# Second block's attention: two weight roundings and their rests moved from the differential heads' steps to the 64-wide heads' steps

## The reference, cut to what matters

```
proj = n @ w_in                           # then split into the parts of three kinds of heads
o_a = mla_causal_attention(...)           # 6 heads, 64 + 32 wide
o_b = diff_causal_attention(...)          # 6 heads, each with two softmaxes over 32-wide halves
o_b = rmsnorm(o_b, sub_norm) * (1 - lam)  # needs all six of them
o_c = moba_causal_attention(...)          # 4 heads, 64 wide; 256 tokens are one block
o = concatenate([o_a, o_b, o_c])
h = h + o @ w_out                         # w_out is 1024 x 1024
h = h + memory_cross_attention(...)       # its keys and values come from another input, mem
```

## Time and profile before

| | us |
|---|---|
| median of 3 runs | 2760.85 |
| lowest and highest | 2758.65, 2761.04 |
| span of the profiled execution | 2767.1 |
| PE busy in it | 2704.7 (98%) |
| DVE busy | 1978.5 (72%) |
| ACT busy | 1665.1 (60%) |

### The profile page before, as it was taken

One profiled execution on the slowest core, in us unless ns is written; L12 is line 12 of the kernel. 1 busy time (PEld: TensorE's weight loads), 2 busy tenths in 40 slices (PEclk: granted clock), 3 DMA queues, 4 the chain that ended last, 5 costly groups with the idle time before them and its releaser, 6 DMA issues. The chain is left out here.

```text
span 2767.1 us, 38903 instructions
## 1 busy us (share of the span) xinstructions
PE 2704.7 (98%) x15424; PEld 2291.4 (83%) x15424; DVE 1978.5 (72%) x2069; ACT 1665.1 (60%) x1965; POOL 86.5 (3%) x86
## 2 busy tenths in 40 slices
PE   8999999999999999999999999999999999999998
PEld 5878999788988888888888888889768998867897
DVE  4756655586779998989899898986655555474555
ACT  3575444558467777777777777766445445354544
POOL 1000100110001000000000000011000000000000
PEclk8999999999999999999999999999999999999999
DMA  9847854865579999999999999986424544414452
GB/s 346 299 139 273 321 203 146 278 226 198 172 289 385 393 377 378 377 374 379 380 374 375 381 373 376 378 276 194 142 92 146 189 183 136 170 62 153 183 190 77
DMA packets 317754, 718.08 MB, mean 260 GB/s; under 512 B 7990, under 2 KB 26916, under 8 KB 317620
## 3 DMA queue, kind: packets, MB, share of 16 engines
q1 hardware_dynamic: 311488, 697.99, 69.5%
q0 software_dynamic: 5520, 18.02, 2.0%
q10 hardware_dynamic: 612, 0.18, 0.0%
HBM read 697.28 MB, written 18.87 MB: 259 GB/s over the span
## 5 line engine op out<-in xcount | busy, mean ns | idle before, releaser
L2775 DVE TENSOR_TENSOR ring_rest<-ring,weights_hi 128x2048 fp32r<-128x2048 f32 x270 | 607.5, 2284 | 9.7 <-ACT weights_hi L2100 7.3
L2100 ACT ACTIVATE weights_hi<-ring 128x2048 fp32r<-128x2048 f32 x270 | 516.6, 1916 | 131.9 <-PE ps L1833 75.7
L1831 PE MATMUL ps<-weights_hi,xg_hi 128*128 128x512 f32 x1008 | 400.9, 398 | 0.7 <-DVE xg_lo L2775 0.7
L1833 PE MATMUL ps<-weights_hi,xg_lo 128*128 128x512 f32 x1008 | 395.0, 392 | 0.0
L1832 PE MATMUL ps<-ring_rest,xg_hi 128*128 128x512 f32 x792 | 310.2, 392 | 0.0
L2100 ACT ACTIVATE arena<-ps 128x512 f32<-128x512 f32 (+6 forms) x307 | 157.3, 529 | 220.0 <-PE ps L1833 54.1
L1852 PE MATMUL ps<-weights_hi,hidden_split_moe 128*128 128x512 f32 x1008 | 284.1, 393 | 1.3 <-DVE hidden_split_moe L2775 1.1
L2775 DVE TENSOR_TENSOR w_split<-ring,w_split 128x1024 fp32r<-128x1024 f32 x128 | 150.9, 1221 | 154.5 <-ACT w_split L2100 154.5
L2775 DVE TENSOR_TENSOR ring_rest<-ring,mix_hi 128x2048 fp32r<-128x2048 f32 (+2 forms) x76 | 173.4, 2284 | 117.2 <-ACT mix_hi L2100 116.7
L2775 DVE TENSOR_TENSOR late_rest<-arena,weights_hi 128x2048 fp32r<-128x2048 f32 x108 | 244.5, 2286 | 5.3 <-ACT weights_hi L2100 4.3
L2100 ACT ACTIVATE weights_hi<-arena 128x2048 fp32r<-128x2048 f32 x108 | 207.0, 1917 | 62.3 <-PE ps L1833 32.5
(11 more groups left out here) (310 smaller groups left out, 5289.5 us busy)
## 6 DMA issues: line engine op xcount, KB each, us to landing
ring<-in_moe_w_gate_dram SPq DMA_DIRECT2D x54, 2048.0 KB, 10.1
ring<-in_moe_w_up_dram SPq DMA_DIRECT2D x45, 2048.0 KB, 10.1
ring<-in_moe_w_down_dram SPq DMA_DIRECT2D x36, 2048.0 KB, 9.2
ring<-in_mlp_w_dram SPq DMA_DIRECT2D x32, 2048.0 KB, 8.8
arena<-in_moe_w_down_dram SPq DMA_DIRECT2D x27, 2048.0 KB, 9.9
ring<-in_w_mod_dram SPq DMA_DIRECT2D x48, 1024.0 KB, 8.8
ring<-in_w_in_dram SPq DMA_DIRECT2D x48, 1024.0 KB, 6.2
arena<-in_moe_w_up_dram SPq DMA_DIRECT2D x18, 2048.0 KB, 10.4
```

The costliest lines, as they stand in the source:

```text
L1831: pe.matmul(b, xg_hi[:, k, :], hi[:, i, :], start=(k == 0), stop=False)
L1833: mm = pe.matmul(b, xg_lo[:, k, :], hi[:, i, :], start=False, stop=(k == KD - 1))
L2100: return act.activation(o, i, func, **kw)
L2775: return dve.tensor_tensor(o, a, b, op)
```

## The change

The two first roundings and rests are issued later in the same loops. Nothing is added or taken away.

```
 # ACT, L2199
-                    if b == 2 and s in (4, 6):
-                        round_2(l, O2_0 + s // 6)
+                    if b == 2 and s in (7, 9):
+                        round_2(l, O2_0 + s // 9)
 # DVE, L2911
-                    if b == 2 and s in (5, 7):
-                        rest_2(l, O2_0 + s // 7)
+                    if b == 2 and s in (8, 10):
+                        rest_2(l, O2_0 + s // 10)
```

## The result

The changed kernel takes 2765.32 us (median of 16 runs, 2761.09 to 2771.94), the kernel before 2760.61 us (16 runs, 2757.01 to 2764.89). The ratio is 1.0017, with a 95% interval of 1.0009 to 1.0024: 4.7 us slower, between 2.5 and 6.6. Forecast were +4.4 us and 2765.3 us, within 0.2% of no change.

A forecast was written before the change was run, and what follows sets the result against it. PE, busy 98% of the span, was taken to bound the kernel. Gain 0 from leaving steps 4 to 7 and 2.2 us cost per layer made 2760.85 + 4.4 = 2765.3 us; range 2758 to 2770.5.

The forecast's parts named there:

- Leaving steps 4 to 7: Taking roundings off ACT in steps 4, 6 and rests off DVE in 5, 7: gain 0, O(3) still waits 0.79 us.
- the fall: PE's granted clock drops from 2.4 to 1.2 GHz after the wait in step 6; priced at 3.14 us per layer.
- The 0.4 us kept for the range: Possible gain per layer at O(4) in step 7, from PT(4)'s copy, only where the clock does not fall.
- The wait at O(7): Step 9's second rounding on ACT delays the copy of PT(7), so PE newly waits 0.98 us at O(7).
- PT(10) 1.8 and O(9) 2.18 us late: Steps 11 and 12, after the second rest on DVE: PT(10) waits 0.85 us more, O(9) is 2.18 us late in all.
- Nothing gives it back: From step 13 on nothing absorbs the delay of about 2 us; distances stay as before from scores(13) on.
- The sum: Both layers' attentions: 2.2 us slower per layer, +4.4 us in all, giving 2765.3 us.
- The 6.3 us between span and median: Median of three runs below the profiled span by 6.3 us, put down to profiler overhead and that execution's clock.
- Rival 1: New waits in steps 10 to 12 make PE's clock fall once more per layer: 6.3 us on top, 2771.6; chance 0.12.
- Rival 2: Step 6's wait goes and the clock stays up: 7.9 us faster, 2753.0, or 2757.4 with the new waits; chance 0.10.
- Rival 3: Everything arriving in steps 7 to 10 finds room, as DVE idles 28% of the span: 0, 2760.9 us; chance 0.16.

The follow-up runs named there:

- the filling: Kernel before, with PE's filling in steps 6, 7, 8, 9, 12, 14, 16, 17 instead of 7, 8, 9, 10, 12, 14, 16, 17: 2756.36 us, ratio 0.9982.
- the small matmuls: Kernel before, with seven more 128 x 128 matmuls on PE in step 6, in front of the wait for O(3): 2757.66 us, ratio 0.9989.
- the rests alone: Kernel before, with only the rests moved, to steps 8 and 10, and the roundings kept in steps 4 and 6: 2762.21 us, ratio 1.0007.
- the roundings behind the copy: Changed kernel, with ACT's roundings of steps 7 and 9 behind their step's copy of PT(s-2): 2761.09 us, ratio 1.0006 to the kernel before.

## Why the prediction was right

**Leaving steps 4 to 7: 0.** Right. O(3) waits 0.80 us in the changed kernel against 0.79, released by ACT, and scores(6) to scores(8) are 11.04 us against 11.05. The rounding and the rest that had stood next to the wait had no part in it; the fall went with the edits on PE, the filling and the small matmuls.

The 0.4 us kept for the range rests on more than the rounding that I named. With the rests alone, layer 1 had no fall and the rounding still in step 6, in front of PT(4)'s copy:

```profile
2438.96 0.57 ACT L2100 ACTIVATE arena<-ps 128x512 f32<-128x512 f32 x1
```

The copy is out at 2439.53, 2.46 us after scores(7), and O(4) starts at 2440.38 without a wait; before it was out 3.66 us after scores(7). The rest of step 5 was gone there, which in the kernel before holds S(6) and with it the exponentials in front of the rounding. It is the chain of O(7), three steps earlier: the kernel before has it too, and in its trace the slow clock hides the 0.4 us.

**The wait at O(7): 0.98 us forecast.** Counted from scores(8), O(7) starts after 11.63 us (2010.68 - 1999.05); before it was 10.68 (2014.89 - 2004.21). That is 0.95. The order rest, S(9), exponentials, rounding, copy is shown by three kernels, each of which breaks the chain at another link and brings the wait to 0.

**PT(10) 1.8 and O(9) 2.18 us late, forecast.** Counted the same way: PT(10) 17.48 us against 15.68, 1.80 late; O(9) 18.36 against 16.21, 2.15 late; the end of the attention 2.21 late, and 2.19 in layer 1. The brackets 0.88, 0.69, 0.22 and 0.23 add up to less, since they count from the end of the last matmul before, and matmuls without a wait start ahead of that end.

**Nothing gives it back.** Right in the sum, and not in one step. I had written the same distances as before from scores(13) on, but scores(14) wait 0.23 us for the copy of PT(10) and start 2.44 us late (2020.32 - 1999.05 against 2023.04 - 2004.21); by PT(13) it is 2.18 us again. The stages behind are unchanged, 289.7 us against 289.6 from the second attention to the end.

**The sum.** +4.4 forecast, +4.45 in the traces, +4.7 by the ratio. That the median came out at 2765.32 is luck to this degree, since the runs spread over 11 us. The falls in step 6 cancelled in the sum: all four in these two kernels were full ones. The 6.3 us between span and median I had put down to the profiler as well; no run shows that. The changed kernel's profiled run took 2765.58 us, close to its median of 2765.32, with a span of 2763.8, 1.8 below its time. With the same 1.8 us, an estimate, the execution with the span of 2767.1 took 2768.9 us, longer than each of the 16 runs.

**Rival 1** (a further fall of the clock) did not happen; windows of PE in the changed kernel, over steps 10 to 12:

```profile
2008.00:2012.00 4.00, 3.12 (x17) 1.00 0.00 0
2012.00:2016.00 4.00, 3.84 (x16) 1.00 0.00 0
2016.00:2018.00 2.00, 1.25 (x10) 1.00 0.02 4
```

The Trainium skill ("TensorE: Matmul & The Clock Gate", section "A second HAM failure mode: psum-queue depth-cycling") tells of a kernel whose clock goes to and fro since PE idles shortly and often between groups of matmuls. That did not happen at the waits of 0.88 and 0.69 us, with fillings in their steps. The clock fell behind the wait of 2.51 us in a step without filling, in both layers, and behind nine of the ten waits of 0.79 us in the thin step 6. **Rival 2** fell because the wait in step 6 stayed. **Rival 3** needed room on DVE that isn't in these steps.

What I had wrong is a price next to the forecast: 3.14 us for a fall, from one trace. It is 0 to 3.3 us by execution. It did not enter the sum, as the fall stayed in both kernels, but it made the expectation for the filling too large.

## What to carry to other kernels

Work that an engine does on the side is free only while the instruction behind it in that engine's queue isn't wanted yet. Write down for each step what stands behind the inserted instruction and when PE wants it; an engine that idles 28% of the span may have no 2.2 us in a given step. When PE waits, ask which queue's order holds its releaser: here three such waits went by swapping two neighbours in a queue or a filling between steps.

## What the runs showed that I had not expected

- The granted clock's fall behind the same 0.79 us wait came in three sizes: 3.3 us in six of ten occurrences, 1.7 in three, 0 in one. The code in front of it was the same for PE in all ten. All four in the two kernels compared cost 3.3 us; the smaller ones came in three kernels that differ from them on ACT or DVE. Ten are too few to tell whether that counts or chance, and so the 2.5 us on average is an estimate for the kernel before too. What decides was not tried.
- In the kernel before, the stretch between the attentions took 363.53 us, in the changed kernel 360.91, with the same waits of PE (7.1 us) and the granted clock at 1.00 in both. In 150 us of it, in which PE was never idle, it issued 980 matmuls in one trace and 1005 in the other:

```profile
2151.00:2301.00 150.00, 150.00 (x980) 1.00 0.49 180
```

```profile
2148.00:2298.00 150.00, 150.00 (x1005) 1.00 0.49 182
```

The first is the kernel before, the second the changed one. The cause stays open. The eight kernels of the experiments took 360.1 to 361.2 us there, so it is the trace of before that stands out, and four of them have the roundings and rests in their old steps, so the change isn't the cause. In the same way the end behind the second attention took 293.05 us with the roundings behind the copy and 288.8 to 289.9 in the nine other traces.
